# Head norms of tiles 0 and 1 in the attention's tail, and the second MLP's bias rows added on chip in the route stage

## The reference, cut to what matters

```
mixed = concat(window attention, RMSNorm per head of the differential attention * gain * 0.8)
h     = x + mixed @ w_out
v     = RMSNorm(h) * g_ffn
logits = v @ w_router + b_router ; top 4 of 32 experts ; gates = softmax of the four
out   = h + sum over the 4 experts of gate * (swiglu(v @ w_mlp1[e] + b_mlp1[e]) @ w_mlp2[e] + b_mlp2[e])
```

## Time and profile before

| | |
|---|---|
| median of 3 runs | 2406.85 us (2403.29 to 2408.19) |
| the profiled execution | 2408.62 us |
| its span, first to last instruction | 2407.0 us |
| mean granted TensorE clock, share of full | 0.975 |
| busy: PE, PEld, DVE, ACT, POOL | 95%, 71%, 78%, 58%, 25% |
| DMA | 520.22 MB, mean 216 GB/s |

### The profile page before, as it was taken

The page is one execution under the profiler, slowest core; times in us unless marked ns, Lnnn a source line. Parts: engine busy times, 40 slices in busy tenths (PEclk is TensorE's granted clock), DMA queues, the critical chain, the costliest instruction groups (busy, mean ns, idle before and its releaser), DMA issues. The chain is left out here.

```text
span 2407.0 us, 34956 instructions
## 1 busy us (share of the span) xinstructions
PE 2281.4 (95%) x10657; PEld 1713.3 (71%) x10658; DVE 1874.5 (78%) x2403; ACT 1399.1 (58%) x1672; POOL 597.5 (25%) x555
## 2 busy tenths in 40 slices
PE   7999998999979949999999999999999999999996
PEld 5778765555538737777777877777777777777775
DVE  4476556989966649888897689797888778989986
ACT  5232455878853426576665466565656556757755
POOL 0133000111101234233241114231223221424423
PEclk9999898999989959999999999999999999999998
DMA  4243812322106559899897679796879777979986
GB/s 163 71 121 107 181 34 87 71 49 58 36 30 158 101 152 345 282 313 330 279 360 233 204 246 373 244 330 228 274 269 329 239 227 255 367 247 364 368 294 225
DMA packets 251776, 520.22 MB, mean 216 GB/s; under 512 B 28642, under 2 KB 60002, under 8 KB 251666
## 3 DMA queue, kind: packets, MB, share of 16 engines
q1 hardware_dynamic: 229522, 480.54, 59.8%
q0 software_dynamic: 22176, 38.70, 7.0%
HBM read 493.59 MB, written 60.15 MB: 230 GB/s over the span
## 5 line engine op out<-in xcount | busy, mean ns | idle before, releaser
L1923 DVE TENSOR_TENSOR wlo<-raw_first,whi 128x2048 fp32r<-128x2048 f32 x259 | 618.3, 2405 | 117.3 <-ACT whi L1810 98.9
L1810 ACT CAST whi<-raw_first 128x2048 fp32r<-128x2048 f32 x259 | 488.9, 1907 | 141.4 <-PE gl_ps L2102 95.0
L2104 PE MATMUL gl_ps<-whi,xt_hi 128*128 128x512 f32 x1056 | 419.3, 397 | 16.1 <-PEq L2148 6.0
L2106 PE MATMUL gl_ps<-whi,xt_lo 128*128 128x512 f32 x1056 | 412.9, 391 | 0.0
L2105 PE MATMUL gl_ps<-wlo,xt_hi 128*128 128x512 f32 x1056 | 412.8, 391 | 0.0
L1923 DVE TENSOR_TENSOR wlo<-raw_later,whi 128x2048 fp32r<-128x2048 f32 x128 | 292.2, 2282 | 59.3 <-ACT whi L1810 59.3
L1810 ACT CAST whi<-raw_later 128x2048 fp32r<-128x2048 f32 x128 | 240.9, 1908 | 68.0 <-PE gl_ps L2102 48.1
L2104 PEld LDWEIGHTS gl_ps<-whi,xt_hi 128*128 128x128 f32 x1056 | 199.1, 189 | 70.0 <-issue 11.8
L1730 POOL DMA_INDIRECT xg<-v_dram,idn x67 | 132.1, 1972 | 395.4 <-PE t_ps L2074 310.6
L2106 PEld LDWEIGHTS gl_ps<-whi,xt_lo 128*128 128x128 f32 x1056 | 199.1, 189 | 43.0
L2105 PEld LDWEIGHTS gl_ps<-wlo,xt_hi 128*128 128x128 f32 x1056 | 199.4, 189 | 40.1
(11 more groups left out here) (299 smaller groups left out, 4068.6 us busy)
## 6 DMA issues: line engine op xcount, KB each, us to landing
raw_first<-in_w_mlp SPq DMA_DIRECT2D x260, 1024.0 KB, 6.8
raw_later<-in_w_mlp SPq DMA_DIRECT2D x130, 1024.0 KB, 6.2
k_st<-qk_dram SPq DMA_DIRECT2D x32, 260.0 KB, 7.5
xs<-in_x SPq DMA_DIRECT2D x16, 512.0 KB, 5.3
w_in_raw<-in_w_in SPq DMA_DIRECT2D x32, 256.0 KB, 3.2
qk_dram<-qk_hi SPq DMA_DIRECT2D x24, 256.0 KB, 2.4
qk_dram<-qk_lo SPq DMA_DIRECT2D x24, 256.0 KB, 2.9
q_st<-qk_dram SPq DMA_DIRECT2D x16, 256.0 KB, 6.6
```

The lines of the kernel that those rows point to most:

```text
L1810: act.copy(whi[:, k % SPL, :], raw(k)).then_inc(hi_done, 1)
L1923: dve.tensor_tensor(wlo[:, k % SPL, :], raw(k), whi[:, k % SPL, :].bitcast(F32), ALU.subtract).then_inc(lo_done, 1)
L2104: pe.matmul(bank, xh[:, half, kc, :], hi, start=start, stop=False, skip_group_check=True)
L2106: return pe.matmul(bank, xl[:, half, kc, :], hi, start=False, stop=stop, skip_group_check=True)
```

## The change

Two things at once.

**Head norms.** A class `HeadNorm` holds what `heads` needs. Its constants and the norms of tiles 0 and 1 move into `attend_diff`: DVE does them right after `store_out(14)`, ACT's two roots stand at the same step. `route` starts with neither a norm nor the scaling of the gain; ACT splits 2 pieces of `w_out` before `copy_mt(0)` (4 before), DVE 1 (4 before).

**Bias rows.** The dense gates of tile u are turned by PE in iteration u+2, after `logits`, into `tv_ps` (shared with `transpose_v`), and split by ACT (96x128) and DVE (32x128). The residual stream of tiles 0 to 5 stays on chip, in `mixed` (in place), that of tiles 6 and 7 in `last_sums`. PE makes the bias rows of tiles 0 to 3 in iteration 7 and of 4 to 7 after it; DVE adds each to its tile (`add_row`, 128x1024); only then does SP store the tile to `sums`: tiles 0 to 5 after the last v, 6 and 7 as the last thing of the block, without waiting for their landing. SP also reads the first slots (`idn`) before the block ends, and it is SP, not POOL, that waits for the scatters. The clearing of `xg` moves to the start of `route`. In `experts` the gate transposes, the 8 products, the 8 copies, the 8 accumulating DMAs and the waits for them are gone; POOL clears `ys` (two writes of 128x1024) after its gathers.

```
@@ attend_diff, scalar and vector @@
+                if back_in(n) == NG - 2:
+                    act.wait_ge(norm.set, 3)
+                    for t in range(norm.AHEAD):
+                        norm.std(act, t)
...
+                if n == U + 1:
+                    dve.wait_ge(weights.landed, 16 * weights.LOADS)
+                    norm.constants(dve)
+                if back_in(n) == NG - 2:
+                    dve.wait_ge(x_copied, use_of[("back", NG - 2)] + 1)
+                    for t in range(norm.AHEAD):
+                        norm.heads(dve, step, t)
@@ route, sync @@
             for t in range(NT):
-                sp.wait_ge(h2_done, 2 * (t + 1))
-                sp.dma_start(sums[t * P:(t + 1) * P, :], h2[:, t % 2, :]).then_inc(h2_sem[t % 2], 16)
...
+            for u in range(NT - 2):
+                store_sum(u)
+            sp.wait_ge(scattered, 16 * NT * TOP_K)
+            sp.dma_start(rows1.idn[:, :, :], slot_dram[0:JOB, :].rearrange("(h p) c -> p h c", p=P)).then_inc(rows1.idx_first, 16)
             for i in range(2):
-                sp.wait_ge(h2_sem[i], 16 * (NT // 2))
                 sp.wait_ge(v_sem[i], 16 * (NT // 2))
+            sp.wait_ge(sums_stored, 16 * (NT - 2))
+            for u in range(NT - 2, NT):
+                store_sum(u)
@@ route, gpsimd @@
+            pool.memset(rows1.xg[:, :, :], 0.0).then_inc(rows_set, 1)
...
-            pool.wait_ge(scattered, 16 * NT * TOP_K)
+            pool.wait_ge(rows_set, 1)
@@ route, vector @@
+            def add_row(u):
+                dve.wait_ge(row_ready, u + 1)
+                dve.wait_ge(v_done, u + 1)
+                dve.tensor_tensor(h2(u).rearrange("p (b n) -> p b n", n=512), row_bank(u),
+                                  h2(u).rearrange("p (b n) -> p b n", n=512), ALU.add).then_inc(row_added, 1)
...
             for t in range(NT + 2):
+                if 3 <= t <= NT:
+                    low_gates(t - 3)
                 if t < NT:
                     residual(t, 0)
...
+                if t == NT - 1:
+                    add_row(0)
+                    add_row(1)
                 if t < NT:
                     residual(t, 1)
+                if t == NT - 1:
+                    for u in range(2, 5):
+                        add_row(u)
+                if t < NT:
                     normalise(t)
...
+                if t == NT:
+                    add_row(NT - 3)
@@ route, tensor @@
+            def turn_gates(u):
+                pe.wait_ge(dense_done, u + 1)
+                pe.wait_ge(vt_done, 2 * min(u + 2, NT - 1))
+                if u >= 1:
+                    pe.wait_ge(gt_low, u)
+                pe.transpose(gt_ps, dense[:, u % 2, :, :].rearrange("p i e -> p (i e)"), ident).then_inc(gt_ready, 1)
```

More of the change, by code:

```diff
@@ L684, in load_head, with attend_diff @@
                 sp.dma_start(buf[rows, :, 0:n].bitcast(F32), src).then_inc(self.st_sem[h % 2], 16)
-def attend_diff(nc, a, v_all, mixed, qk_dram, early_win, stacks, weights):
+def attend_diff(nc, a, v_all, mixed, qk_dram, early_win, stacks, weights, norm):
     with ExitStack() as ctx:
@@ L1186, in _, with route @@
                     act.copy(ot[:, u % 2, :], o_ps[0:DV, :]).then_inc(ot_done, 1)
-def route(nc, a, mixed, gates, picks, jobs, bias, sums, v_dram, slot_dram, weights):
+def route(nc, a, mixed, gates, picks, jobs, rows1, sums, v_dram, slot_dram, weights, norm):
     with ExitStack() as ctx:
@@ L1575, in _, with experts @@
             pe.matmul(r_ps[0:1, 128 + 2 * NJ:128 + 3 * NJ], ec[:, 2:3], ej[:, 2, :], start=True, stop=True).then_inc(cnt_ready, 1)
-def experts(nc, a, first, bias, jobs, v_dram, slot_dram, sums):
+            bias_row(NT - 1)
+def experts(nc, a, first, rows1, jobs, v_dram, slot_dram, sums):
     with ExitStack() as ctx:
@@ L1605, in experts @@
         b1 = sb("b1", [P, 2 * D])
-        idn = sb("idn", [P, 2, 2], U32)
+        idn = rows1.idn
         idm = sb("idm", [P, 2, 2], U32)
         idc = sb("idc", [P, 2, 2], U32)
-        ident = bias.ident
-        rows = sb("bias_rows", [P, OWN, 2, 512])
-        ys_parts = lambda half: ys[:, half, :].rearrange("p (c n) -> p c n", n=512)
-        stage = [sg[:, :, :], lin[:, :, :], hh[:, :, :], ys_parts(0), ys_parts(1), *[rows[:, i, :, :] for i in range(OWN)]]
+        ident = rows1.ident
         gl_ps = ps("gl_ps", [P, 2, 2, 512])
@@ L1894, in body @@
                     finish(j, half, kind)
-            act.wait_ge(gt_ready, 1)
-            act.copy(gates_p, t_ps[0:3 * N_EXP, :, :].rearrange("e b n -> e (b n)")).then_inc(gt_copied, 1)
             for k in range(AHEAD):
                 split(0, k)
-            for t in range(0, NT, 2):
-                act.wait_ge(b_ready, t + 1)
-                act.copy(stage[t], bias_banks(t)).then_inc(b_copied[0], 1)
             keep_x0(0)
@@ L2227, in build @@
                 weights = RouteWeights(nc, late, first)
-                attend_diff(nc, a, v_all, mixed, qk_dram, early_win, stacks, weights)
-            bias = BiasRows(nc, whole)
-            route(nc, a, mixed, gates, picks, jobs, bias, sums, v_dram, slot_dram, weights)
-        experts(nc, a, first, bias, jobs, v_dram, slot_dram, sums)
+                norm = HeadNorm(nc, late, mixed, weights)
+                attend_diff(nc, a, v_all, mixed, qk_dram, early_win, stacks, weights, norm)
+            rows1 = FirstRows(nc, whole)
+            route(nc, a, mixed, gates, picks, jobs, rows1, sums, v_dram, slot_dram, weights, norm)
+        experts(nc, a, first, rows1, jobs, v_dram, slot_dram, sums)
 def rope_table():
```

271 lines of the change are left out of this document (150 added, 121 removed).

## The result

The changed kernel took 2379.19 us (median of 4 runs, 2376.72 to 2382.78) where the kernel before took 2406.31 beside it: ratio 0.9885, 95% interval 0.9873 to 0.9896, so 27.1 us faster. Two later measurements gave 2379.51 (2378.01 to 2386.56) and 2379.83 (2378.39 to 2380.55), ratios 0.9891 and 0.9883. The direction was right. The size was not: I had said 2387.6, and 2380 to 2398.

What follows compares the result with a forecast made beforehand. PE bounds the expert loop, so an earlier first product there moves the end equally. -9.5 + 2.2 + 1.4 - 1.45 - 11.9 = -19.25 from the median 2406.85 gives 2387.6 us; range 2383 to 2393, with rivals 1 and 2 2380 to 2398.

Steps and rivals of the forecast that it cites:

- A: Start of the route stage: with two head norms moved into DVE's earlier gap, PE's first w_out product comes sooner; -9.5 us.
- B: Route stage up to tile 7's last product: PE gains five turned gate tiles and two bias rows; +2.2 us.
- C: Ahead of `normalise(7)`: DVE adds three bias rows where it waited 2.82 us for ACT; +1.4 us.
- D: From `normalise(7)` to the last `dsti`: tile 7's transposes of v come ahead of `ranks(6)`, so `logits(7)` starts sooner; -1.45 us.
- E: From the last `dsti` to PE's first product of the expert loop: 26.9 us where it was 38.8; -11.9 us.
- Stores in the way of the scatters: End of route stage: bunched stores delay the last scatters and the gather, leaving a gain of 10, 2397 us; chance 0.17.
- The clock stays up: Route stage's end and start: bias rows in PE's idle time may keep its clock from halving, 2383 us; chance 0.15.
- Cover in the loop gone: Expert loop: weight loads pace the first jobs, so E's gain is lost, 2399.5 us, or 2403 with last stores; chance 0.05.
- Turned gates close a loop: Route tiles 2 to 7: `transpose_v` waits for earlier gates' round trip, PE stands still, slower at 2421 us; chance 0.04.

Runs made afterwards that it cites:

- heads alone: Kernel before, with only the norms of tiles 0 and 1 moved into the attention's tail and the bias rows as before: 2395.54 us, ratio 0.9952.

## Why the prediction was right and wrong

**What bounds the kernel**: right. PE is as busy in the loop as before, so what PE's start gained the end gained. The loop was 2.2 to 3.0 us shorter in the three profiles than in the one of the kernel before, but with the heads alone, whose loop and loop's start are the old ones, it was as short (1509.9), so no gain in the loop is shown. What can be explained of the error is in when PE could start.

**A, the head norms: right**, -9.5 forecast, -10.0 measured (9.5 at w_out's first product, 0.5 behind it in the first tile, of which I had 0.2 for the second norm; the first tile's scatter of 0.6 makes that 0.5 uncertain). The cover was enough, with 0.1 us left rather than 1.4: ACT's table load (1.28) stood between the norm's sum and its root, and I had priced both norms by one that had no table load ahead of it.

**B, PE's added work: mis-sized**, +2.2 forecast, +0.8 measured. Five turned gates, for which I took 1.0, cost nothing that the distances show, and some 0.2 with the shorter wait counted in. A pair of products costs 0.4 to 0.5 where I took 0.6: I had halved the 1.22 of a pair standing alone at the low clock, start to end, and in a full queue the next product starts before the pair's row ends.

**C, the additions: direction right, size off**, +1.4 forecast, +0.8 measured: the last one waited 0.22 for PE, not some 0.5 and more.

**D: right**, -1.45 forecast, -1.5 measured.

**E, from the last `dsti` to the loop: the step that failed**, -11.9 forecast, -15.4 to -17.1 measured (39.0 less 23.6 to 21.9). Its parts: the gather issued 12.5 us after the end of `dsti`, measured 11.5, 12.2 and 13.2, right; its landing 7.9, measured 4.4, 4.6 and 4.3, wrong by 3.3 to 3.6; transposes and 5.0 us of sequencer to the first product 6.5, measured 5.9, 5.6 and 6.0. I had taken the landing from the gathers of that stretch in the trace (7.7 and 8.5 for the two at this place), and had not asked what they ran beside: the weight loads had been issued 0.9 us ahead of the first, and the change put it 1.4 to 1.6 ahead of them. The run with the loads first gives 2.9 to 3.2 of it back, nearly all. The two last stores, for which I had allowed up to 3 us, did not hold the gather up, though they were moving when it was issued. I had also kept the 5.0 us of sequencer as a term of its own. Its two reads were 1.9 us shorter and done while DVE was still splitting, and DVE's third split, which I let "run meanwhile", was the bound. That the two nearly cancelled is luck.

Summed, B (1.4), C (0.6), A (0.5) and E (3.5 to 5.2) are 6.0 to 7.7 of the 7.85 us between forecast and measured gain (19.25 and 27.1). The bound of E on the side of a larger gain, -13.4, was too tight: only a shorter sequencer was allowed for in it, and a landing taken from a crowded case needs a bound below as well.

**Rivals.** Stores in the way of the scatters: no. The burst was over by 843, and the slots were read 8.9 to 10.6 us after `dsti`, where the kernel before had them landed by 9.8 (its drain starts at 865.8). The clock stays up: no, 0.50 up to the loop, and the first 3.6 us of w_out products at 0.50 in either kernel. Cover in the loop gone: no, PE is busy 1427.54 of 1464 us. Turned gates close a loop: no, tiles 1 to 6 take 88.9 us with and without them.

## What to carry to other kernels

A DMA's duration in a trace belongs to its neighbours as much as to itself: before moving one, look at what was issued just ahead of it, and bound its price from below by a case in which nothing bulky was issued just ahead. An issue moved early enough to pass the bulk loads can gain more than the time it was moved by, and one moved late can lose more (the read of the slots at the next block's start cost 5.6 to 7.3 here). Compare distances that leave out the stretch in which the clock rises: over the whole stage the price of two pairs read 0.6 us, tile by tile 1.0. Extra work for an engine is best put into a wait that ends in another engine's hands, and no further: behind that wait stands work that others need.

## What the runs showed of the hardware

- A gather of 128 rows of 4 KB: 4.3 to 4.6 us from issue to its first user when the weight loads were issued 1.4 to 1.6 us behind it (in the changed kernel's first profile 1 MB of stores was still moving at the issue, DMA share 1.00 from 856 to 857), 7.5 when 1 MB weight loads had been issued ahead of it, 8.9 when its issue also fell into a DVE split (issue 2.70 us against 1.05).
- That issue ended 0.9 us after the end of the DVE split that it met, in both runs where it met one.
- POOL's drain at a block's end takes 2.76 us if the indirect DMAs have landed; started ahead of their landing it still ends 1.4 us behind it.
- Four scatters of 128 pairs each are seen landed 8.9 to 10.6 us after the indices in executions of the same kernel. This alone can move the loop's start by 1.7 us.
- A pair of 96-row products within PE's full queue cost 0.4 to 0.5 us at full clock, and 1.22 from start to end at half clock standing alone.
- PE's two register reads of the job list took 1.3 to 1.75 us each in the kernels that still had the accumulating stores under way, 0.49 and 0.32 in those without, even beside weight loads. The cause is open.
